# Attention's opening in a hybrid encoder block: the trunk's output buffer in another order, the exponential's table loaded ahead, the later keys split in two pieces

## The chip, the cores and the metric

The kernel runs on one core of a Trainium2 chip. A core has five engines with instruction streams of their own: TensorE (matrix products and transposes), VectorE, ScalarE (activation functions), GpSimd, and SyncE, which here only issues transfers. They are ordered by semaphores alone. In profile rows they are PE (PEld for its weight loads), DVE, ACT, POOL and SP; SPq and ACTq are the issues of transfers from the queues of SyncE and ScalarE. The metric is the device time of one execution in microseconds.

## The reference

One layer of a streaming encoder for a prompt of 2048 positions and a sample of 32 new positions on 1024 past ones. Everything is float32.

```python
(aq, ak, av, iq, ik, iw, za, uv, zb, glu, zc, gates) = split_columns(rms_norm(x, norm_g) @ w_in)
...
o_a = dsa_prompt(q, iq, iw, k, v, ik)                      # or dsa_attend with the cache
o_b, v_rows = gmlp_unit(uv, g_ln_g, g_ln_b, g_ws, g_bs)
o_c, conv_tail = conv_module(glu, left, c_w, c_b, c_ln_g, c_ln_b)
merged = (ga * ((o_a * jax.nn.silu(za)) @ w_a) + gb * ((o_b * jax.nn.silu(zb)) @ w_b)
          + gc * ((o_c * jax.nn.silu(zc)) @ w_c))
x = x + merged @ w_out
x = x + jax.nn.sigmoid(rms_norm(x, ple_g) @ w_pg) * (p @ w_ple)
```

The part in question is `dsa_attend`: 8 query heads of width 64 share 2 key and value heads, each query sees the 256 keys that an indexer selected, with a distance penalty per head:

```python
logits = jnp.einsum('btgrd,btkgd->btgrk', qg, kg).astype(jnp.float32) * (A_HEAD_DIM ** -0.5)
logits = logits - slopes[None, None, :, :, None] * dist[:, :, None, None, :]
logits = jnp.where(valid[:, :, None, None, :], logits, -jnp.inf)
prob = jax.nn.softmax(logits, axis=-1).astype(v.dtype)
out = jnp.einsum('btgrk,btkgd->btgrd', prob, vg)
```

## The kernel before, in words

The trunk (`stage_trunk`) multiplies the normed input with w_in in 59 jobs of 128 columns, each over five spans of 416 positions. Each float32 operand is split into a high and a low part, and a product is three matmuls. ScalarE copies each span from PSUM to its place in `j_out` (`evacuate`), span r to place r, and stores it to `T_dram`; from the third job on spans 0 and 1 go in one store and spans 2 to 4 in another. The last job stores 0 and 1, then 2 and 3, then 4, with a semaphore of its own for the last (`last_stored`). `stored[1]` counts the first kind, `stored[4]` the second.

Attention (`stage_attend`) follows. It works in 34 groups: a group is one tile of queries and one of the two key heads (four query heads), in the order of tiles 0, 3, 4, 1, 5, 2, 6, 7 and so on; tile t sees 128 (t + 1) keys. For each head of a group TensorE multiplies queries and keys (lines 2417 and 2418), VectorE adds the distances and takes the running minimum in one pass into the buffer `a_l` (line 2547), ScalarE takes the exponential in place (line 2473), TensorE transposes 128 columns of four heads at a time (line 2374), ScalarE copies the high part (`a_pthi`, line 2482), VectorE makes the low part (`a_ptlo`, line 2571), and TensorE multiplies with the values (lines 2438 and 2439). Three PSUM banks go round for products and three for transposes. Products, minima and exponentials of a group are done beside the transposes and values of the group before it. The sums' reciprocals (lines 2559 and 2563) go through DRAM: SyncE stores them (`share`, line 2137) and loads them broadcast as `a_factor` (line 2143); GpSimd multiplies them with the gates and the output (lines 2258 and 2264). SyncE also loads the queries (`a_q`, lines 148 and 149) and the distances (`a_nd`, line 2166), and GpSimd splits the queries (lines 2249 and 2251). All of this stands in a fixed order on each engine's queue.

`a_l` of head 0 begins at byte 163584 of each partition, `j_out` at byte 157440, with 1664 bytes to a place. So the first 512 columns of head 0's `a_l` lie over places 3 and 4 of `j_out`, and no other head's does. The first product's minimum (group 0, head 0) therefore waits for stores of `j_out` (`wait_for_outputs`), and the first of group 2 also for the last store. One of the two queries buffers lies over the other places and is loaded by SyncE, which waits for all stores first.

Keys are split into high and low parts by ScalarE (a cast, `high`, line 2455) and VectorE (a subtraction, `split`, line 2513): the first 512 of each key head ahead of group 0, the other 1536 at the starts of groups 2 and 3; the values of the later positions at those of groups 5 and 6. `SPLITS_AT` holds this table. The buffers with the raw later keys (`a_krest`) lie in the columns from 512 on of `a_l` of heads 4 and 5.

Of the kernel before, what the change touches and what calls it, by code (L numbers as in the profile page):

```python
# [45 lines left out]
SPAN = 416  # L46
# [1304 lines left out]
def stage_trunk(c):  # L1351
# [68 lines left out]
    kv_stored = c.kv_stored  # L1420

    w_in = c.I["w_in"].rearrange("(k q) n -> q k n", q=P)
    w_second = out[:].rearrange("q b t -> q (b t)")[:, 0:D].rearrange("q (k n) -> q k n", k=KD)
    pT = [c.psum[:, 2 * p:2 * p + 2, :].rearrange("q b (k t) -> q (b k) t", k=4) for p in range(4)]
    turn_bank = lambda t: t if t in GROUPS[0] else t % 2
# [26 lines left out]
    c.wait_for_products = lambda eng: eng.wait_ge(bank_full, finished(SLOTS - 1))  # L1452
    c.wait_for_banks_read = lambda eng, b: eng.wait_ge(bank_read, sequence(SLOTS - 1, b) + 1)
    c.wait_for_outputs = lambda eng: wait_for_stored(eng, SLOTS - 1)
    c.wait_for_last_output = lambda eng: eng.wait_ge(last_stored, 16)
    c.wait_for_early = lambda eng: (eng.wait_ge(product, IH * len(parts(NS))), eng.wait_ge(nat_stored, 32))

# [105 lines left out]
    def scalar(act):  # L1563
# [19 lines left out]
        def evacuate(j, b):  # L1583
            q = sequence(j, b)
            r, slot, t0 = q % len(SPANS), JOBS[j][1], SPANS[b][0]
            act.wait_ge(bank_full, q + 1)
            if j < 2:
                if q == 0:
                    act.wait_ge(w_lo_done, 2)
                if q >= len(SPANS):  # L1590
                    act.wait_ge(stored[r], 16)
            elif j == 2:
                act.wait_ge(stored[r], 32)
            else:
                act.wait_ge(stored[1 if b < 2 else 4], 16 * j)
            if S_Q <= slot < S_K:
                c.wait_for_scale(act)
                act.activation(out[:, r, :], c.psum[:, bank_of(j, b), 0:SPAN], ACT.Identity, scale=c.scale[:, slot - S_Q:slot - S_Q + 1]
                               ).then_inc(bank_read, 1)
            else:  # L1600
                act.activation(out[:, r, :], c.psum[:, bank_of(j, b), 0:SPAN], FUNC[JOBS[j][2]]).then_inc(bank_read, 1)  # L1601
            if j < 2:
                act.wait_ge(bank_read, q + 1)
                act.dma_start(c.T_dram[slot, :, t0:t0 + SPAN], out[:, r, :]).then_inc(stored[r], 16)
            elif b in ((1, 3, 4) if j == SLOTS - 1 else (1, 4)):
                first, end = HELD[0 if b == 1 else 1]
                sem = stored[1 if b == 1 else 4]
                if j == SLOTS - 1 and b > 1:
                    first, end, sem = (first, 4, sem) if b == 3 else (4, end, last_stored)
                act.wait_ge(bank_read, q + 1)  # L1610
                act.dma_start(c.T_dram[slot, :, first * SPAN:end * SPAN], out[:, first:end, :].rearrange("q b t -> q (b t)")
                              ).then_inc(sem, 16)

        def relu(n):
# [338 lines left out]
def stage_attend(c):  # L1953
# [379 lines left out]


    splits = [(k_hi[g][:, 0:FIRST_KEYS], k_lo[g][:, 0:FIRST_KEYS], kraw[g][:], (c.k_full, 64)) for g in range(KVH)]
    splits += [(k_hi[g][:, FIRST_KEYS:], k_lo[g][:, FIRST_KEYS:], krest[g][:], (c.rest_full[g], 32)) for g in range(KVH)]
    for g in range(KVH):
        dst = v_p[:, HALF:, g, :]
        splits.append((dst[:, :, 0:HD], dst[:, :, HD:P], vraw[1][:, :, g * HD:(g + 1) * HD], (values_full, 16)))

    SECOND_ROWS_AT = ((last_prompt, 12), (groups[-1], 2))
    SPLITS_AT = {2: (2,), 3: (3,), 5: (4,), 6: (5,)}

    WIDE = next(group for group in groups if len(group.tiles) > HALF)
    assert WIDE.n > 7
    FIRST_KEYS_SPLIT, KEYS_SPLIT, VALUES_SPLIT = 1, 3, 5

    late_splits = [(ks_hi[g][:, PAST:], ks_lo[g][:, PAST:], new_k[g][:], P) for g in range(KVH)]
    for g in range(KVH):
# [13 lines left out]
    def tensor(pe):  # L2363
# [26 lines left out]
        def unit(group, unit):  # L2390
# [7 lines left out]
            if s == 0 and h == group.buffers[0]:  # L2398
                if group.n == 0:
                    c.wait_for_first_queries(pe)  # L2400
                    c.wait_for_early_cleared(pe)
                    c.wait_for_banks_read(pe, QK - 1)
                if group.i == 1:
                    c.wait_for_second_queries(pe)
                if group.i > 1:
                    pe.wait_ge(q_ready[group.p], splits_of_queries(group.i) + 1)
                if group.i == 1:
                    pe.wait_ge(operands, FIRST_KEYS_SPLIT + group.g)
                if group.i == 2:
                    pe.wait_ge(operands, KEYS_SPLIT + group.g)  # L2410
                if group.t == DT:
                    pe.wait_ge(late_ready, len(late_splits))
                    pe.wait_ge(cache_ready, len(CACHE_GROUPS))
# [37 lines left out]
    def scalar(act):  # L2451
# [8 lines left out]

        c.wait_for_early_cleared(act)
        c.wait_for_products(act)

        def first():
            high(0)
# [43 lines left out]
    def vector(vec):  # L2509
# [13 lines left out]
        def unit(group, unit):  # L2523
            h, s, a, w, b, nb, n = unit
            if n == 0:
                c.wait_for_swish_spans(vec)
                c.wait_for_outputs(vec)
            if n == 6:
                c.wait_for_swish(vec)
            if unit is groups[KVH].units[0]:  # L2530
                c.wait_for_last_output(vec)
            n_d = c.nd_first if group.i == 0 else nd[group.p]
            if s == 0 and group.packed:
                vec.wait_ge(rs_cleared, 1 + 4 * KVH)
# [1354 lines left out]
```

## Time and profile before

| | us |
|---|---|
| median of 3 executions | 2644.74 (2643.83 to 2645.25) |
| the profiled execution, its own time | 2642.72 |
| its span | 2640.7 |
| TensorE busy in it | 2591.1 (98%) |
| VectorE busy | 2054.9 (78%) |
| ScalarE busy | 1496.6 (57%) |
| GpSimd busy | 1537.0 (58%) |

The span is the time from the first to the last instruction of the profiled execution; its own time is 2.0 us longer. All positions in time below are microseconds from the span's start. The trunk's last matmul starts at 1530.79; attention's last groups end at about 1965. Busy time of TensorE is modelled for a pipeline, so 98% does not say that no faster order of the work exists. A row of a timeline gives the start, the duration, the engine, the line, the operation, what it writes and reads, and in brackets the idle time in front of it with what ended it.

### The profile page before, as it was taken

The page shows a single profiled execution, that of the slowest core. Times are in us where ns is not written, and L with a number is a line of the kernel's source. Part 1 is how long each engine was busy: PE and PEld are TensorE (multiplying, and loading weights), DVE is VectorE, ACT ScalarE, POOL GpSimd, SP SyncE. Part 2 cuts the span into 40 slices and gives each one's busy share as a digit, 9 for nine tenths or more (in the row PEclk, how much of TensorE's full clock was granted, in tenths as well). Part 3 has the DMA queues.
Part 4 walks back from the last instruction along what each step waited for, and adds up shares of the span by engine and source line. Part 5 has one row for each costly group of instructions (what it writes and reads, how often), then busy time and mean ns, then how long its engine had stood idle before and what let it go on. Part 6 is the DMA issues. An engine that isn't in the chain of part 4 may idle for free. (4 is left out here: it accounts for less than half of the span.)

```text
span 2640.7 us, 40128 instructions
## 1 busy us (share of the span) xinstructions
PE 2591.1 (98%) x13799; PEld 2410.3 (91%) x13799; DVE 2054.9 (78%) x3857; ACT 1496.6 (57%) x2550; POOL 1537.0 (58%) x1114
## 2 busy tenths in 40 slices
PE   8999999999999999999999988999999999999998
PEld 8999999999999999999999967878889999877886
DVE  6377799999999999998363568999977666657656
ACT  6377578686868787785222367777760101326553
POOL 1100187787878796889345558543347663976562
PEclk9999999999999999999999989999999999999999
DMA  5433333233433332323465564222138976642221
GB/s 181 129 118 128 120 102 118 99 114 109 132 107 122 99 122 88 114 88 123 132 209 167 178 171 115 80 66 70 54 129 316 351 264 212 230 158 100 95 85 57
DMA packets 279959, 359.94 MB, mean 136 GB/s; under 512 B 37905, under 2 KB 227985, under 8 KB 279117
## 3 DMA queue, kind: packets, MB, share of 16 engines
q1 hardware_dynamic: 171667, 219.73, 26.0%
q10 hardware_dynamic: 108090, 137.66, 15.0%
q8 instruction: 110, 1.80, 0.3%
q14 instruction: 92, 0.75, 0.1%
HBM read 216.94 MB, written 139.74 MB: 135 GB/s over the span
## 5 line engine op out<-in xcount | busy, mean ns | idle before, releaser
L1762 PE MATMUL psum<-hT_hi,j_whi 128*128 128x416 f32 x2432 | 864.9, 356 | 1.6 <-ACT j_out L1601 0.8
L1762 PE MATMUL psum<-hT_hi,j_wlo 128*128 128x416 f32 x2432 | 852.7, 351 | 0.0
L1762 PE MATMUL psum<-hT_lo,j_whi 128*128 128x416 f32 x2432 | 851.6, 350 | 0.0
L1314 POOL TENSOR_TENSOR v_y<-v_y,v_product 128x422 f32<-128x422 f32 x459 | 562.9, 1264 | 88.9 <-ACT v_product L1296 88.9
L449 DVE TENSOR_SCALAR_CACHE_REDUCE s_tie<-s_key,s_bits 128x640 bf16<-128x640 f32 (+14 forms) x352 | 464.3, 1319 | 12.3
L1762 PEld LDWEIGHTS psum<-hT_hi,j_whi 128*128 128x128 f32 x2432 | 456.2, 188 | 11.2 <-issue 2.6
L1762 PEld LDWEIGHTS psum<-hT_lo,j_whi 128*128 128x128 f32 x2432 | 457.4, 188 | 9.0 <-issue 1.6
L1762 PEld LDWEIGHTS psum<-hT_hi,j_wlo 128*128 128x128 f32 x2432 | 456.2, 188 | 5.5
L1296 ACT ACTIVATE v_product<-v_x,v_taps 128x422 f32<-128x422 f32 x510 | 303.1, 641 | 81.4 <-POOL v_y L1314 58.7
L1601 ACT ACTIVATE j_out<-psum 128x416 f32<-128x416 f32 x285 | 144.9, 509 | 323.4 <-PE psum L1762 312.2
L1521 POOL TENSOR_TENSOR j_wlo<-j_w,j_whi 128x1024 fp32r<-128x1024 f32 x59 | 143.8, 2437 | 313.8 <-ACT j_whi L1581 313.8
L2482 ACT ACTIVATE a_pthi<-psum 128x512 fp32r<-128x512 f32 x278 | 161.8, 596 | 91.9 <-PE psum L2374 90.1
L432 ACT ACTIVATE s_ajunk<-s_key,s_abits,s_asign 128x1280 uint8<-128x1280 bf16 (+7 forms) x112 | 192.4, 1718 | 14.0 <-ACT j_out L1601 11.0
L2571 DVE TENSOR_TENSOR a_ptlo<-psum,a_pthi 128x512 fp32r<-128x512 f32 x278 | 186.2, 682 | 11.1 <-ACT a_pthi L2482 10.9
L2374 PEld LDWEIGHTS psum<-ident,a_l 128*128 128x128 f32 x1106 | 133.1, 141 | 53.4 <-DVE a_ptlo L2571 25.3
L2374 PE MATMUL psum<-ident,a_l 128*128 128x128 f32 x1106 | 166.0, 276 | 13.5 <-DVE a_ptlo L2571 9.0
L3205 PE MATMUL psum<-f_whi,f_ahi 128*128 128x512 f32 x448 | 177.2, 395 | 1.1 <-issue 0.9
L3205 PE MATMUL psum<-f_wlo,f_ahi 128*128 128x512 f32 x448 | 174.7, 390 | 0.0
L3205 PE MATMUL psum<-f_whi,f_alo 128*128 128x512 f32 x448 | 174.5, 389 | 0.0
L2764 PE MATMUL psum<-m_ohi,m_wlo 128*128 128x416 f32 x480 | 169.4, 353 | 0.0
L2764 PE MATMUL psum<-m_ohi,m_whi 128*128 128x416 f32 x480 | 168.3, 351 | 0.8 <-issue 0.8
L2764 PE MATMUL psum<-m_olo,m_whi 128*128 128x416 f32 x480 | 167.5, 349 | 0.0
(372 smaller groups left out, 4947.0 us busy)
## 6 DMA issues: line engine op xcount, KB each, us to landing
T_dram<-j_out ACTq DMA_DIRECT2D x58, 624.0 KB, 2.9
j_w<-in_w_in ACTq DMA_DIRECT2D x59, 512.0 KB, 3.8
T_dram<-j_out ACTq DMA_DIRECT2D x60, 416.0 KB, 2.4
m_gate<-T_dram SPq DMA_DIRECT2D x60, 416.0 KB, 5.6
m_oraw<-B_dram SPq DMA_DIRECT2D x15, 832.0 KB, 8.6
M_dram<-m_merged ACTq DMA_DIRECT2D x10, 832.0 KB, 7.1
n_x<-in_x_prompt SPq DMA_DIRECT2D x16, 512.0 KB, 6.1
G_dram<-f_prepsums ACTq DMA_DIRECT2D x8, 1024.0 KB, 5.6
```

Of the source, the lines that this page charges most:

```text
L432: do(act.activation(a_junk[:, 0:n], tops, ACT.Sign, scale=a_sign[:, p:p + 1], bias=level, accum_out=a_cnt))
L449: do(vec.tensor_scalar(tie[:, 0:n], K[:, 0:n], bits[:].bitcast(F32), 0.0, ALU.is_ge, ALU.add, accum_out=cnt[:]))
L1296: act.activation(product[n % RING][:], x, ACT.Identity, scale=taps[:, k:k + 1]).then_inc(made, 1)
L1314: pool.tensor_tensor(y[k % 2][:], y[k % 2][:], product[n % RING][:], ALU.add).then_inc(added, 1)
L1521: pool.tensor_tensor(w_lo[j % 2][:], w_raw[:], f32(w_hi[j % 2][:]), ALU.subtract).then_inc(w_lo_done, 1)
L1601: act.activation(out[:, r, :], c.psum[:, bank_of(j, b), 0:SPAN], FUNC[JOBS[j][2]]).then_inc(bank_read, 1)
L1762: last = pe.matmul(bank, w[p][:, k, :], h[:, k, t0:t0 + SPAN], start=(k == 0 and q == 0), stop=(k == KD - 1 and q == 2))
L2374: last = pe.transpose(c.psum[0:w, PT[u], r * P:(r + 1) * P], L[h][:, block * P:block * P + w], c.ident[:])
L2482: act.activation(pT_hi[number % KEPT][0:w, 0:n], c.psum[0:w, PT[u], 0:n], ACT.Copy).then_inc(pt_hi, 1)
L2571: vec.tensor_tensor(pT_lo[number % KEPT][0:w, 0:n], c.psum[0:w, PT[u], 0:n], f32(pT_hi[number % KEPT][0:w, 0:n]), ALU.subtract).then_inc(p ...
L2764: last = pe.matmul(c.psum[:, n, 0:SPAN], wt[:, k, n * P:(n + 1) * P], o[u][:, k, :], start=(k == 0 and q == 0), stop=(k == 3 and q == 2))
L3205: last = pe.matmul(out, left[:, k, :], right[:, k, :], start=(k == 0 and x == 0), stop=(k == KH - 1 and x == 2))
```

## The change

Three edits. The output buffer's places are turned by three: span r lies at place (r + 3) mod 5, so spans 0 and 1 lie at places 3 and 4, and spans 2, 3, 4 at 0, 1, 2. The first minimum waits for `stored[0]` and `stored[1]` only, and the wait ahead of group 2 goes. ScalarE runs an exponential of one column into a constant that is not needed any more, as soon as the trunk's products are finished. The 1536 later keys are split 512 (up to position 1024) and 1024: the first piece where it was, the second at the starts of groups 12 and 13, ahead of the first group that needs it (tile 8, group 16).

```diff
+    place = lambda r: (r + 3) % len(SPANS)
...
+    c.wait_for_first_outputs = lambda eng: (eng.wait_ge(stored[0], 32), eng.wait_ge(stored[1], 16 * SLOTS))
...
-                act.activation(out[:, r, :], c.psum[:, bank_of(j, b), 0:SPAN], FUNC[JOBS[j][2]]).then_inc(bank_read, 1)
+                act.activation(out[:, place(r), :], c.psum[:, bank_of(j, b), 0:SPAN], FUNC[JOBS[j][2]]).then_inc(bank_read, 1)
...
-                act.dma_start(c.T_dram[slot, :, first * SPAN:end * SPAN], out[:, first:end, :].rearrange("q b t -> q (b t)")
+                act.dma_start(c.T_dram[slot, :, first * SPAN:end * SPAN], out[:, place(first):place(end - 1) + 1, :].rearrange("q b t -> q (b t)")
...
-    splits += [(k_hi[g][:, FIRST_KEYS:], k_lo[g][:, FIRST_KEYS:], krest[g][:], (c.rest_full[g], 32)) for g in range(KVH)]
+    NEAR = SEQ // 2
+    piece = lambda g, a, b: (k_hi[g][:, a:b], k_lo[g][:, a:b], krest[g][:, a - FIRST_KEYS:b - FIRST_KEYS], (c.rest_full[g], 32))
+    splits += [piece(g, FIRST_KEYS, NEAR) for g in range(KVH)]
...
+    splits += [piece(g, NEAR, SEQ) for g in range(KVH)]
...
-    SPLITS_AT = {2: (2,), 3: (3,), 5: (4,), 6: (5,)}
+    SPLITS_AT = {2: (2,), 3: (3,), 5: (4,), 6: (5,), 12: (6,), 13: (7,)}
+    FAR_KEYS = next(group for group in groups if group.keys > NEAR)
...
+                if group.i == FAR_KEYS.i:
+                    pe.wait_ge(operands, FAR_SPLIT + group.g)
...
         c.wait_for_early_cleared(act)
         c.wait_for_products(act)
+        act.activation(c.scale[:, 0:1], c.zero[:], ACT.Exp)
...
             if n == 0:
                 c.wait_for_swish_spans(vec)
-                c.wait_for_outputs(vec)
+                c.wait_for_first_outputs(vec)
             if n == 6:
                 c.wait_for_swish(vec)
-            if unit is groups[KVH].units[0]:
-                c.wait_for_last_output(vec)
```

ScalarE at the end of the trunk, before: the last store, the table's load, the exponentials of group 0.

```order
L1601 ACTIVATE j_out<-psum 128x416
L1611 DMA T_dram<-j_out 128x416
L2473 ACT_TABLE_LOAD
L2473 ACTIVATE a_l_232,a_sums<-a_l_232,a_lows 128x128
L2473 ACTIVATE a_l_233,a_sums<-a_l_233,a_lows 128x128
```

And in the changed kernel:

```order
L1603 ACTIVATE j_out<-psum 128x416
L1613 DMA T_dram<-j_out 128x416
L2472 ACT_TABLE_LOAD
L2472 ACTIVATE scale<-zero 128x1
L2483 ACTIVATE a_l_232,a_sums<-a_l_232,a_lows 128x128
L2483 ACTIVATE a_l_233,a_sums<-a_l_233,a_lows 128x128
```

The table's load now belongs to the one-column activation, whose operands are there, and no longer to the first exponential, which waits for the first minimum.

VectorE at the start of group 12, before: the low part of the group's first transposed block, reciprocal and its transpose, then minima (two rows each) and low parts by turns.

```order
L2571 TENSOR_TENSOR a_ptlo_248<-psum,a_pthi_244 128x512
L2559 RECIPROCAL a_rs<-a_sums 128x4
L2563 STREAM_TRANSPOSE a_rsT_260<-a_rs 128x32
L2547 ISA a_l_237,a_lows<-psum,a_nd_230,a_lows 128x448
L2547 ISA a_lows 128x1
L2571 TENSOR_TENSOR a_ptlo_249<-psum,a_pthi_245 128x512
```

And in the changed kernel:

```order
L2579 TENSOR_TENSOR a_ptlo_248<-psum,a_pthi_244 128x512
L2523 TENSOR_TENSOR a_klo_222<-a_krest_174,a_khi_220 128x1024
L2567 RECIPROCAL a_rs<-a_sums 128x4
L2571 STREAM_TRANSPOSE a_rsT_260<-a_rs 128x32
L2555 ISA a_l_237,a_lows<-psum,a_nd_230,a_lows 128x448
L2555 ISA a_lows 128x1
L2579 TENSOR_TENSOR a_ptlo_249<-psum,a_pthi_245 128x512
```

One subtraction of 1024 columns has come in ahead of the reciprocal; group 13 has another at the same place, and the corresponding rows of groups 2 and 3 read 128x512 where they read 128x1536. SyncE's, GpSimd's and TensorE's rows stand in the order of before.

## Rows read from the trace of the kernel before

**Rows 1.** Windows: us, then busy us and instructions by engine, granted clock, DMA.

```profile
1534.00:1548.00 14.00, 11.99 (x36) 8.69 (x37) 10.48 (x34) 10.42 (x31) 9.24 (x6) 0.52 0.59 151
...
1640.00:1660.00 20.00, 19.69 (x113) 15.91 (x112) 18.79 (x48) 16.62 (x32) 15.28 (x11) 1.00 0.45 122
```

**Rows 2.** Timeline of the opening: start, duration, engine, operation, idle time in front.

```profile
1531.73 0.35 ACTq L1611 DMA_DIRECT2D T_dram<-j_out  x1
...
1533.62 0.29 DVE L2547 CUSTOM_DVE_ANT_0 a_l<-psum,a_ndfirst 128x128 f32<-128x128 f32 x1 [7.83 <-DMA T_dram<-j_out]
...
1534.02 1.28 ACT L2473 ACT_TABLE_LOAD   x1 [2.32 <-DVE a_lows L2547]
...
1537.90 0.59 ACT L2482 ACTIVATE a_pthi<-psum 128x512 fp32r<-128x512 f32 x1
```

**Rows 3.** The store of 1527.2, the last swish store's issue, SyncE's wait behind it.

```profile
L1611 ACTq DMA_DIRECT2D T_dram<-j_out x1: 327/327/327, 1527.2 to 1527.2; - x1
...
DMA to landing us min/median/max: 5.9/5.9/5.9
...
1525.15 0.51 SPq L902 DMA_DIRECT2D B_dram<-w_y  x1
...
SPq L925 <- DMA B_dram<-w_y: 6.7, 1, 6.7
```

**Rows 4.** Source view, lines 2513 and 2455: ns min/median/max, first and last start.

```profile
L2513 DVE TENSOR_TENSOR a_klo<-a_kraw,a_khi x2: 970/1366/1762, 1537.6 to 1538.5; 128x512 fp32r<-128x512 f32 x2
L2513 DVE TENSOR_TENSOR a_klo<-a_krest,a_khi x2: 1747/2072/2396, 1550.3 to 1561.1; 128x1536 fp32r<-128x1536 f32 x2
L2513 DVE TENSOR_TENSOR a_vp<-a_vraw,a_vp x2: 682/784/887, 1577.3 to 1584.2; 128x512 fp32r<-128x512 f32 x2
...
L2455 ACT CAST a_khi<-a_kraw x2: 602/608/613, 1536.9 to 1537.4; 128x512 fp32r<-128x512 f32 x2
L2455 ACT CAST a_khi<-a_krest x2: 1456/1466/1475, 1547.6 to 1556.9; 128x1536 fp32r<-128x1536 f32 x2
```

**Rows 5.** Timeline at group 2's start, VectorE and GpSimd.

```profile
1549.73 0.69 DVE L2571 TENSOR_TENSOR a_ptlo<-psum,a_pthi 128x512 fp32r<-128x512 f32 x1 [1.42 <-ACT a_pthi L2482]
...
1549.85 1.27 POOL L2264 TENSOR_TENSOR a_oa<-a_oa,a_factor 64x512 f32<-64x512 f32 x1
...
1550.33 2.40 DVE L2513 TENSOR_TENSOR a_klo<-a_krest,a_khi 128x1536 fp32r<-128x1536 f32 x1
```

**Rows 6.** SyncE's issues in order of time; last, the values' landing.

```profile
1538.14 0.43 SPq L2182 DMA_DIRECT2D a_vraw<-out_v_prompt  x1
1540.60 1.27 SPq L2137 DMA_DIRECT2D RS_dram<-a_rsT  x4
1545.64 0.47 SPq L2143 DMA_DIRECT2D a_factor<-RS_dram  x1
...
1562.90 0.64 SPq L149 DMA_DIRECT2D a_q<-T_dram  x1
...
1583.28 0.59 SPq L2166 DMA_DIRECT2D a_nd<-ND_dram  x1
...
a_vraw<-out_v_prompt SPq DMA_DIRECT2D x1, 512.0 KB, 6.8
```

**Rows 7.** Timeline: what waits for these queries and distances.

```profile
1567.17 1.90 POOL L2249 TENSOR_TENSOR a_qs<-a_q,zero 128x1024 fp32r<-128x1024 f32 x1 [10.25 <-DMA a_q<-T_dram]
...
1587.16 0.56 DVE L2547 CUSTOM_DVE_ANT_0 a_l<-psum,a_nd 128x384 f32<-128x384 f32 x1 [0.94 <-DMA a_nd<-ND_dram]
```

**Rows 8.** Timeline at group 12's start; last, a wait of VectorE in 1628 to 1652.

```profile
1628.62 1.28 POOL L2273 TENSOR_TENSOR a_oa<-a_oraw,a_oa 64x512 f32<-64x512 f32 x1
...
1629.53 0.17 DVE L2559 RECIPROCAL a_rs<-a_sums 128x4 f32<-128x4 f32 x1
...
1630.12 0.68 DVE L2547 CUSTOM_DVE_ANT_0 a_l<-psum,a_nd,a_lows 128x448 f32<-128x448 f32 x1 [0.17 <-PE psum L2418]
...
DVE a_ptlo L2571 <- ACT a_pthi L2482: 0.3, 1, 0.3
```

More of the change, by code:

```diff
@@ L1597, in evacuate @@
                 c.wait_for_scale(act)
-                act.activation(out[:, r, :], c.psum[:, bank_of(j, b), 0:SPAN], ACT.Identity, scale=c.scale[:, slot - S_Q:slot - S_Q + 1]
+                act.activation(out[:, place(r), :], c.psum[:, bank_of(j, b), 0:SPAN], ACT.Identity, scale=c.scale[:, slot - S_Q:slot - S_Q + 1]
                                ).then_inc(bank_read, 1)
             else:
-                act.activation(out[:, r, :], c.psum[:, bank_of(j, b), 0:SPAN], FUNC[JOBS[j][2]]).then_inc(bank_read, 1)
+                act.activation(out[:, place(r), :], c.psum[:, bank_of(j, b), 0:SPAN], FUNC[JOBS[j][2]]).then_inc(bank_read, 1)
             if j < 2:
                 act.wait_ge(bank_read, q + 1)
-                act.dma_start(c.T_dram[slot, :, t0:t0 + SPAN], out[:, r, :]).then_inc(stored[r], 16)
+                act.dma_start(c.T_dram[slot, :, t0:t0 + SPAN], out[:, place(r), :]).then_inc(stored[r], 16)
             elif b in ((1, 3, 4) if j == SLOTS - 1 else (1, 4)):
@@ L2339, in stage_attend @@
         splits.append((dst[:, :, 0:HD], dst[:, :, HD:P], vraw[1][:, :, g * HD:(g + 1) * HD], (values_full, 16)))
+    splits += [piece(g, NEAR, SEQ) for g in range(KVH)]
     SECOND_ROWS_AT = ((last_prompt, 12), (groups[-1], 2))
-    SPLITS_AT = {2: (2,), 3: (3,), 5: (4,), 6: (5,)}
+    SPLITS_AT = {2: (2,), 3: (3,), 5: (4,), 6: (5,), 12: (6,), 13: (7,)}
+    FAR_KEYS = next(group for group in groups if group.keys > NEAR)
+    assert FAR_KEYS.g == 0 and FAR_KEYS.n - KVH > 13
     WIDE = next(group for group in groups if len(group.tiles) > HALF)
     assert WIDE.n > 7
-    FIRST_KEYS_SPLIT, KEYS_SPLIT, VALUES_SPLIT = 1, 3, 5
+    FIRST_KEYS_SPLIT, KEYS_SPLIT, VALUES_SPLIT, FAR_SPLIT = 1, 3, 5, 7
     late_splits = [(ks_hi[g][:, PAST:], ks_lo[g][:, PAST:], new_k[g][:], P) for g in range(KVH)]
```

## The prediction

> **What bounds the kernel now.** The windows view by stretches comes first. From 1534 to 1548 us, the opening of attention, TensorE is granted 0.52 of its clock (almost wholly its 1.2 GHz level) and nobody is full; from 1640 to 1660 TensorE is busy 19.69 and VectorE 18.79 of 20 us [rows 1]. So the opening is a chain of waits, and later attention runs two full engines in step. Behind attention everything is ordered by semaphores and nothing starts at a fixed time, so what attention gains or loses is the change of the total.
>
> The timeline of the opening shows the first minimum starting at 1533.62 after 7.83 us of idle time that a store of j_out ended; the exponential's table is loaded from 1534.02, for 1.28 us, once that minimum is there; the first a_pthi copy starts at 1537.90 [rows 2].
>
> The timeline of SyncE and GpSimd is where I spent most time, because an opening that gets faster has to be fed. SyncE issues the second half of the values at 1538.14 (6.8 us to landing), the first reciprocal stores at 1540.60, the first factor load at 1545.64, the second half of the fourth tile's queries at 1562.90 and the distances of the fifth tile at 1583.28 [rows 6]. GpSimd idles 10.25 us until those queries have landed, at 1567.17; VectorE idles 0.94 us at 1587.16 for those distances, which had been issued only 3.9 us before [rows 7].
>
> **The change part by part.**
>
> *Fewer stores to wait for.* The first minimum no longer waits for the store that carries spans 2 and 3 of the last job. That store was issued at 1527.2 and landed 5.9 us later, 1533.1 [rows 3]; VectorE moved 0.5 us behind it. What is late next is the wait that stays in the same instruction's list, for the swish stage's stores: SyncE issued the last of these until 1525.66 and then waited 6.7 us, until 1532.36 [rows 3]. With the same 0.5 us behind it the first minimum starts at 1532.9, 0.7 us earlier. Bounds: 0 (if the swish stores land later than here) and 1.3 (no lag at all). The wait for the last span's store, dropped before the second tile's minima, cost nothing: they run some microseconds later than it lands. The buffer's other order moves no instruction in the trunk and keeps each store one contiguous piece: nothing either way.
>
> *Table ahead.* ScalarE is free from 1532.08, when its last store is issued (1531.73 plus 0.35) [rows 2]. The table stands at 1533.4 instead of 1535.30. The added one-column activation is shorter than the 0.61 us of a 512-column cast [rows 4] and lies where ScalarE idled. The exponentials can start 1.5 us earlier or so, but TensorE still has five pairs of products to run behind the first minimum before it transposes, and these move by 0.7 only. The first a_pthi copy, which needs both, moves between 0.7 and 1.7 us; I take 1.3.
>
> *Later keys in two pieces.* In groups 2 and 3 (each group is a tile and half of the heads) the cast takes 0.61 instead of 1.47 us, the subtraction 0.68 (the 512-column values piece without anything beside it) instead of 2.40 and 1.75 [rows 4]. In group 2 VectorE had waited 1.42 us for the a_pthi copy that stands behind the cast, so these 0.86 us pass through, then 2.40 - 0.68 = 1.72; in group 3 I count 1.75 - 0.68 = 1.07 in full (its lower bound is 0). Gross gain of the opening: 1.3 + 0.86 + 1.72 + 1.07 = 4.95 us by 1563.
>
> *What is late next.* None of these 4.95 us is in SyncE's and GpSimd's chain. Its links from 1540.60 on are: reciprocals landing, factor load at 1545.64, ten more issues, reciprocals again, queries at 1562.90, GpSimd from 1567.17 with hardly a pause (one split of queries, two groups of gates), a store of attention's output, reciprocals, distances at 1583.28. In it I find waits for transfers and for GpSimd, and one for VectorE, at its head: the 1540.60 issue. If VectorE arrives 1.3 us earlier there, the four small stores go out 1.3 us earlier, but behind 512 KB of values issued at 1538.14 that landed at 1544.94; SyncE went on at 1545.64, 0.7 us behind that landing and 3.8 us behind its own last small store (1540.60 plus 1.27) [rows 6]. So I let this chain move by 0.3 us (bounds 0 and 1.3). The minimum at 1587.16 is the first to read those distances and VectorE runs in order. Whatever the opening gained above 0.3 us is waited away there.
> The Trainium skill (DMA: Bandwidth & Descriptors, section Queues, rings and completion order) says that a ring's descriptors are consumed in order and that a semaphore's increment lands after the engine's earlier writes. By it the chain would move by 0; with a fixed latency from issue it would be the 1.3.
>
> *The pieces that come back.* Two casts and two subtractions of 1024 columns now stand at the starts of groups 12 and 13, at 1629.53 and some 11 us later. No row shows that width; halfway between 0.68 (512) and 1.75 (1536) is 1.21 us, which is the lower bound. The subtraction at 1550.33 began while GpSimd ran an operation from 1549.85 to 1551.12, and ended at 1552.73, 1.6 us after that end [rows 5]: it stood still first. At 1628.62 GpSimd starts 1.28 us of the same sort, so group 12's piece would stand still until 1629.90, 0.37 us [rows 8]. For group 13 the bounds are 0 and the 1.90 us of GpSimd's queries operation [rows 7]; I take 0.8. Together 2 x 1.21 + 0.37 + 0.8 = 3.6 us (bounds 2.4 and 6.2).
> The Trainium skill (SBUF — State Buffer, section Who interferes with whom) says that a VectorE instruction with two SBUF inputs and a GpSimd instruction that reads SBUF lock each other out, the second one waiting for the whole of the first. The four short pieces and the long ones here agree with that; by the rule with no such overlap the sum would be 2.4.
> What hides them? Behind the place in group 12 VectorE idles 0.17 us, and over 1628 to 1652 it waited 0.3 us for ScalarE [rows 8]: 0.5 us. TensorE waits for the a_ptlo right behind it, and has itself no more than some tenths to spare [rows 1]. So 3.1 us come through (bounds 1.2, with every microsecond of VectorE's idle time used, and 6.2). The casts, about 1.0 us, fit into ScalarE's waits.
>
> *Sum.* -0.3 + 3.1 = +2.8 us; I shade this to +2.5, since queue slack that rows don't show can only help. The profiled execution took 2642.72 us, so 2645.2; the median before is 2644.74, 2.0 above it, so 2647.2 us as measured.
>
> **The rivals.**
> - *The factor chain moves with VectorE.* Fixed latency, 1.3 us instead of 0.3: +1.5 us, 2646.2. For it: the 3.8 us after the issue's end are long and named as a wait for these stores alone. Against it: the landing of the values 0.7 us before.
> - *The late pieces are hidden.* VectorE's busy 18.79 of 20 leave 1.2 us; if the rings between TensorE and VectorE take up both pieces, what remains is some 0.5 us: +0.2, 2644.9. Against: TensorE is full too, and it waits for this very engine.
> - *Faster: the distances at 1583.28 are not what holds.* This is one mechanism: SyncE's chain gives way to an earlier VectorE, because its links are shorter with less traffic beside them. It decides from the point where it moves by more than 3.1 us; were all 4.95 us passed on, the time would be 4.95 - 3.1 = 1.9 us below before, 2642.8. For it: the wait at 1587.16 is only 0.94 us. Against: each link is a transfer or a GpSimd operation that no edit touches.
> - *Clock.* The opening ran at the 1.2 GHz level behind a lull of TensorE. Waiting for 1587 makes TensorE's lull longer and could drop it again. With TensorE busy nine tenths of the time later on [rows 1], 4 us at half rate lose 2 us of products, 2649.2. The reverse (a shorter lull at 1532 keeps the clock up) gains nothing at 1587.
>
> **How the numbers follow.** Forecast 0.45, factor chain 0.15, hidden pieces 0.15, faster 0.15, clock 0.10. The range from 2642.6 to 2649.6 reaches from the faster case to the clock's; beyond it lie the bound of 6.2 us and a part of the faster case. 0.2% is 5.3 us, about what a measurement of this kernel can tell from no change. No case's centre is that far: faster 0.02, same 0.94, slower 0.04. Inside it only one case, of 0.15, lies below before.
>
> **What would show it.** First minimum near 1532.9 and the table load before it; in groups 2 and 3 subtractions of 0.7 to 1 us; SyncE's factor load still within 0.5 us of 1545.64 and the distances within 1 us of 1583.28; a VectorE wait for a_nd of 2 us or more before 1587; the 1024-column pieces at 1.2 us or, beside GpSimd, up to 3, with TensorE waiting behind them. I am wrong if the distances are issued 2 us earlier, or if group 14 starts no later than before.

## The result and the profile after

The kernel before takes 2643.59 us in the runs that share a chip with the changed one (median of 20), the changed kernel 2647.76 us (median of 20, 2645.97 to 2654.89). The ratio is 1.0015 with a 95% interval of [1.0009, 1.0022], so the change costs 4.0 us, between 2.4 and 5.8. One of the 20 executions of before took 4109.26 us; the ratio is formed of fast runs alone, without it. The forecast was 2647.2 us, +2.5. The profiled executions took 2648.93 us after and 2642.72 before.

The windows view of the changed kernel: us, then busy us and instructions of PE, PEld, DVE, ACT and POOL, granted clock, DMA share, GB/s.

```profile
1534.00:1548.00 14.00, 11.28 (x43) 7.75 (x42) 10.31 (x32) 10.30 (x33) 9.71 (x8) 0.76 0.63 157
1570.00:1580.00 10.00, 7.03 (x30) 6.18 (x31) 4.88 (x13) 4.25 (x9) 9.22 (x10) 0.66 0.32 90
1640.00:1660.00 20.00, 17.26 (x92) 13.70 (x91) 17.44 (x40) 13.26 (x25) 14.27 (x10) 0.91 0.24 65
```

The kernel before from 1570 to 1580:

```profile
1570.00:1580.00 10.00, 8.59 (x54) 6.67 (x53) 9.15 (x27) 9.33 (x22) 8.05 (x10) 1.00 0.43 115
```

Against [rows 1] the opening has a higher clock, 0.76 for 0.52. There is a new hole from 1570 to 1580, where VectorE is busy for 4.88 of 10 us instead of 9.15 and the clock is 0.66 instead of 1.00, and a second one from 1640 to 1660, where TensorE falls from 19.69 to 17.26 of 20 and its clock from 1.00 to 0.91.

The opening's timeline, as [rows 2]. In this execution attention's first product starts at 1532.07 and in that of before at 1530.98, so 1.09 us have to be taken off each start before the two are compared.

```profile
1532.81 0.35 ACTq L1613 DMA_DIRECT2D T_dram<-j_out  x1
1533.21 0.29 DVE L2555 CUSTOM_DVE_ANT_0 a_l<-psum,a_ndfirst 128x128 f32<-128x128 f32 x1 [6.34 <-SPq L925]
1533.25 1.28 ACT L2472 ACT_TABLE_LOAD   x1 [0.47 <-ACT j_out L1603]
...
1534.54 0.20 ACT L2472 ACTIVATE scale<-zero 128x1 f32<-128x1 f32 x1
...
1536.04 0.29 DVE L2555 CUSTOM_DVE_ANT_0 a_l<-psum,a_ndfirst 128x128 f32<-128x128 f32 x1 [0.87 <-SPq L927]
...
1537.22 0.58 ACT L2492 ACTIVATE a_pthi<-psum 128x512 fp32r<-128x512 f32 x1
```

The table no longer waits for a minimum, and the first copy to a_pthi comes 5.15 us after the first product instead of 6.92. The first minimum comes 1.14 us after it instead of 2.64. What releases the first minimum is now SyncE's wait for the swish stores (L925), and its wait for the tails (L927) holds the seventh for another 0.87 us.

Groups 2 and 3, as [rows 4, 5]: the new 512-column pieces.

```profile
1548.30 0.69 DVE L2579 TENSOR_TENSOR a_ptlo<-psum,a_pthi 128x512 fp32r<-128x512 f32 x1 [0.89 <-ACT a_pthi L2492]
...
1548.91 0.68 DVE L2523 TENSOR_TENSOR a_klo<-a_krest,a_khi 128x512 fp32r<-128x512 f32 x1
...
1557.81 0.68 DVE L2523 TENSOR_TENSOR a_klo<-a_krest,a_khi 128x512 fp32r<-128x512 f32 x1
```

Then SyncE, GpSimd and VectorE, as [rows 6, 7]: the links of the chain and the waits that end it.

```profile
1540.05 2.06 SPq L2139 DMA_DIRECT2D RS_dram<-a_rsT  x4
1546.32 0.47 SPq L2145 DMA_DIRECT2D a_factor<-RS_dram  x1
...
1563.90 1.53 SPq L149 DMA_DIRECT2D a_q<-T_dram  x1
...
1568.60 1.90 POOL L2251 TENSOR_TENSOR a_qs<-a_q,zero 128x1024 fp32r<-128x1024 f32 x1 [11.84 <-DMA a_q<-T_dram]
...
1572.97 0.58 PE L2426 MATMUL psum<-a_khi,a_qs 128*128 128x256 f32 x1 [3.71 <-POOL a_qs L2253]
...
1575.23 0.42 DVE L2555 CUSTOM_DVE_ANT_0 a_l<-psum,a_nd 128x256 f32<-128x256 f32 x1 [3.67 <-PE psum L2427]
...
1584.61 0.59 SPq L2168 DMA_DIRECT2D a_nd<-ND_dram  x1
...
1588.70 0.56 DVE L2555 CUSTOM_DVE_ANT_0 a_l<-psum,a_nd 128x384 f32<-128x384 f32 x1 [1.01 <-DMA a_nd<-ND_dram]
```

Counted from the first product, the factor load comes 0.41 us earlier than before and the distances 0.24 us later. The chain has hardly moved, so VectorE, which was 5.5 us ahead at group 3's reciprocal, stands still for 3.67 us at 1575 and twice more by 1588.70. TensorE idles 3.71 us there for the queries that GpSimd is splitting, and its clock falls behind that lull: this is the 0.66 of the window. Part of the lead is lost to slower products, then, and not to the wait itself. At 1588.70 it is 1.54 us behind before's 1587.16, of which 1.09 is the later start.

The starts of groups 12 and 13, as [rows 8]:

```profile
1631.12 1.24 DVE L2523 TENSOR_TENSOR a_klo<-a_krest,a_khi 128x1024 fp32r<-128x1024 f32 x1
1631.24 2.27 POOL L2260 TENSOR_TENSOR a_factor<-a_factor,a_za 64x512 f32<-64x512 f32 x1
1632.28 0.17 DVE L2567 RECIPROCAL a_rs<-a_sums 128x4 f32<-128x4 f32 x1
...
1642.33 1.89 POOL L2251 TENSOR_TENSOR a_qs<-a_q,zero 128x1024 fp32r<-128x1024 f32 x1
1642.64 2.66 DVE L2523 TENSOR_TENSOR a_klo<-a_krest,a_khi 128x1024 fp32r<-128x1024 f32 x1
1644.30 3.22 POOL L2253 TENSOR_TENSOR a_qs<-a_q,a_qs 64x1024 fp32r<-64x1024 f32 x1
...
1647.03 1.08 PE L2381 MATMUL psum<-ident,a_l 128*128 128x128 f32 x4 [2.61 <-DVE a_ptlo L2579]
```

The piece of group 12 takes 1.24 us. That of group 13 begins 0.31 us behind a GpSimd operation that reads SBUF, and ends 1.08 us after that one's end: it stood still first. TensorE then idles 2.61 us, and its next four products (transposes, line 2381) take 1.08 us.

Reciprocals of group 8, counted from the first product, and the stretch from there to group 14's are the two measures used below. Before: 67.43 and 52.21 us. After: 67.90 and 57.16. Nearly all of the loss lies in the second, 4.95 us against 0.47. Both are measures of one execution each.

### The profile page after: what moved, and what is told of

It is laid out like the page before. It is cut to its first block and busy times, and to the rows that moved or that the text cites. A ratio compares the mean times of both kernels' runs of the same rounds, so it can differ in the third digit from the quotient of the medians.

```text
span 2647.1 us, 40131 instructions
## 1 busy us (share of the span) xinstructions
PE 2592.4 (98%) x13799; PEld 2411.2 (91%) x13799; DVE 2060.4 (78%) x3859; ACT 1496.2 (57%) x2553; POOL 1538.3 (58%) x1114
## 5 line engine op out<-in xcount | busy, mean ns | idle before, releaser
L1523 POOL TENSOR_TENSOR j_wlo<-j_w,j_whi 128x1024 fp32r<-128x1024 f32 x59 | 149.4, 2532 | 321.4 <-ACT j_whi L1583 321.4
```

The lines of the kernel that those rows point to most:

```text
L1523: pool.tensor_tensor(w_lo[j % 2][:], w_raw[:], f32(w_hi[j % 2][:]), ALU.subtract).then_inc(w_lo_done, 1)
```

## The experiments

All were timed in five rounds against the kernel before on the same chip; "against before" is worked out from the ratio and its interval. Theory A is the prediction's: the opening's gain is waited away, and the loss is the late pieces.

**1. The change without the split of the keys.**

```
-    splits += [piece(g, FIRST_KEYS, NEAR) for g in range(KVH)]
+    splits += [(k_hi[g][:, FIRST_KEYS:], k_lo[g][:, FIRST_KEYS:], krest[g][:], (c.rest_full[g], 32)) for g in range(KVH)]
...
-    splits += [piece(g, NEAR, SEQ) for g in range(KVH)]
...
-    SPLITS_AT = {2: (2,), 3: (3,), 5: (4,), 6: (5,), 12: (6,), 13: (7,)}
+    SPLITS_AT = {2: (2,), 3: (3,), 5: (4,), 6: (5,)}
```

> The change without its split of the keys: the output places, the wait for two stores and the early load of the table stay, the keys beyond the first 512 are made in one piece per group again. Theory A (the opening's gain of the first minima and of the table, 1.5 to 1.8 us here, is waited away by 1589 at the queries and distances of the third and fourth tile, and the loss comes from the 1024-column pieces at groups 12 and 13): 2643.6, no further than 1 us from before; the idle time of VectorE between 1568 and 1589 is 1 to 2 us larger than before's. Theory B (the changed order of the output buffer costs the trunk 1 us, as the later first product in the profile of after suggests): +1 us, with the first product of attention 1 us later than before's 1530.98 again. Theory C (the opening's gain survives and only the split costs): -1.3 us, 2642.3.

Measured: 2643.31 us, ratio 1.0001 [0.9992, 1.001], +0.3 us (-2.1 to +2.6). Its first minimum:

```profile
1534.81 0.29 DVE L2548 CUSTOM_DVE_ANT_0 a_l<-psum,a_ndfirst 128x128 f32<-128x128 f32 x1 [8.08 <-SPq L925]
```

It comes 2.89 us after its first product, no earlier than before's 2.64, though the wait for the j_out store is gone: the swish store landed later here. The first product is at 1531.92, which looked like theory B, but in six of the later kernels with the same output places it is at 1530.31 to 1531.02. In two others, numbers 5 and 10, it is at 1536.00 and 1535.29; in the four profiled executions with the old places it is at 1530.79 to 1531.26. So theory B has no support in the time, whose interval does hold its +1, and it is not excluded. The stretch from group 8 to 14 is 52.21 us. Group 8's reciprocal is at 68.29 us, 0.86 later than before's, so nothing of the opening's gain is left there. Theory A stands; C's -1.3 lies inside the interval of the time.

**2. The split alone, on the kernel before.**

```
+    splits += [piece(g, NEAR, SEQ) for g in range(KVH)]
...
-    SPLITS_AT = {2: (2,), 3: (3,), 5: (4,), 6: (5,)}
+    SPLITS_AT = {2: (2,), 3: (3,), 5: (4,), 6: (5,), 12: (6,), 13: (7,)}
```

> The kernel before with the split of the keys alone: pieces of 512 at groups 2 and 3, of 1024 at groups 12 and 13. Theory A: the whole loss is here, +3.5 to +4.5 us over before (2647 to 2648), with the sum of VectorE's piece at group 13 stretched to over 2.3 us while GpSimd splits queries, and group 14's reciprocal 4.5 to 5.5 us later than before's. Theory B (the trunk pays): +2.5 to +3. Theory D (the 5.8 us seen at group 14 in the one profile was an accident of that execution's clock; pieces cost their bare 1.2 us each): +1 to +2.

Measured: 2649.12 us, ratio 1.0017 [1.0008, 1.0025], +4.5 us (+2.1 to +6.6). Groups 8 to 14 take 57.36 us, 5.15 more than before; group 14's reciprocal is 6.9 us later than before's, where A said 4.5 to 5.5. A wait takes the gain of groups 2 and 3:

```profile
1587.35 0.56 DVE L2554 CUSTOM_DVE_ANT_0 a_l<-psum,a_nd 128x384 f32<-128x384 f32 x1 [3.81 <-DMA a_nd<-ND_dram]
...
1642.85 2.66 DVE L2520 TENSOR_TENSOR a_klo<-a_krest,a_khi 128x1024 fp32r<-128x1024 f32 x1
```

The whole loss is in the split, as A said. Theory D's +1 to +2 is out.

**3. The late pieces at groups 10 and 12.**

```
-    SPLITS_AT = {..., 12: (6,), 13: (7,)}
+    SPLITS_AT = {..., 10: (6,), 12: (7,)}
```

> The change, with the two 1024-column pieces put at groups 10 and 12 in place of 12 and 13, so that neither begins beside GpSimd's split of queries, which runs at odd groups. If the lock at group 13 and the lull behind it are what cost (theory A): each piece takes 1.2 to 1.3 us on VectorE, no wait of TensorE over 1.5 us follows either, the TensorE clock stays at 1.00, and the time is +2 to +2.7 over before instead of +4. If the cost is a piece's bare work on a full VectorE (theory D): as after, within 0.5 us (+3.5 to +4.5).

Measured: 2646.60 us, ratio 1.0012 [1.0003, 1.002], +3.2 us (+0.8 to +5.3). The profile tells more than the time:

```profile
1615.18 1.85 DVE L2523 TENSOR_TENSOR a_klo<-a_krest,a_khi 128x1024 fp32r<-128x1024 f32 x1
...
1630.71 2.12 DVE L2523 TENSOR_TENSOR a_klo<-a_krest,a_khi 128x1024 fp32r<-128x1024 f32 x1
```

Neither piece took the 1.2 to 1.3 us expected, since GpSimd has shorter operations at even groups too, and TensorE waited 1.67 and 1.74 us behind them where no wait over 1.5 was expected. But the clock stays at 1.00 in 1640 to 1660 and groups 8 to 14 take 55.04 us, 2.1 less than in after. The expectation for the pieces was wrong. The interval of the time holds A's loss of 2 to 2.7 and D's of 3.5 to 4.5 alike; the profile's 2.8 us over before in groups 8 to 14 lies by A's.

**4. The fourth tile's queries loaded earlier.**

```
             share(sp, first)
-            if 0 < i < TILES - 2:
+            if 1 < i < TILES - 2:
                 load_queries(i + 2)
...
+            if i == 0:
+                load_queries(3)
             share(sp, second)
```

> The change, with the third tile's queries loaded by SyncE in the first tile's shares instead of behind the second tile's (their buffer is free from the start), so GpSimd splits them some 10 us earlier. Theory A (at 1575 the products of the fourth tile in order wait for these queries, which hold back what the opening gained): the 3.67 us wait of VectorE at 1575 goes or falls under 1 us; the distances at 1588 then hold, with a wait longer by as much unless their load is also earlier; time 0 to 2.5 us below after (+1.5 to +4 over before), the low clock around 1575 gone. Rival (the distances alone hold, as the prediction had it): the wait moves whole to 1588 and the time is after's within 0.5 us.

Measured: 2647.53 us, ratio 1.0015 [1.0006, 1.0024], +4.0 us (+1.6 to +6.3).

```profile
1575.02 0.42 DVE L2557 CUSTOM_DVE_ANT_0 a_l<-psum,a_nd 128x256 f32<-128x256 f32 x1 [3.98 <-DMA a_nd<-ND_dram]
...
1642.43 2.67 DVE L2525 TENSOR_TENSOR a_klo<-a_krest,a_khi 128x1024 fp32r<-128x1024 f32 x1
...
1646.84 0.63 PE L2383 MATMUL psum<-ident,a_l 128*128 128x128 f32 x4 [2.61 <-DVE a_ptlo L2581]
```

Neither expectation was met: the wait did not go, and it did not move to 1588. It keeps its place and nearly its size, but what ends it is now the fourth tile's distances: SyncE issues those behind the same shares of reciprocals. Both queries and distances had been late by about 4 us. By accident this execution also measures the clock. After the same piece and the same lull of 2.61 us, TensorE's four products take 0.63 us where after's took 1.08; the clock in 1640 to 1660 is 1.00, and group 13's to group 14's reciprocal takes 10.36 us against 11.90 in after (10.38 in before).

**5. The late pieces put into the wait, at group 4** (the list of pieces is put in the same order).

```
-    SPLITS_AT = {2: (2,), 3: (3,), 5: (4,), 6: (5,), 12: (6,), 13: (7,)}
+    SPLITS_AT = {2: (2,), 3: (3,), 4: (4, 5), 5: (6,), 6: (7,)}
```

> The change, with both 1024-column pieces put at the start of group 4 (about 1566), ahead of the 4 to 5 us in which VectorE waits around 1571 to 1577 for the fourth tile in order. Theory A (the opening's gain is waited away there, so that stretch has room): the two pieces fill the wait, VectorE's wait at 1575 falls from 3.67 us to under 1.5, groups 12 to 14 run as before, and the time is before's within 1 us (-1 to +1). Rival (the pieces delay what the SyncE chain itself waits for, group 4's reciprocal at 1566 and group 5's at 1579): +3 to +5, the wait at 1588 grown.

Measured: 2643.55 us, ratio 0.9999 [0.999, 1.0008], -0.3 us (-2.6 to +2.1).

```profile
1570.33 2.35 DVE L2523 TENSOR_TENSOR a_klo<-a_krest,a_khi 128x1024 fp32r<-128x1024 f32 x2
...
1580.04 0.69 DVE L2579 TENSOR_TENSOR a_ptlo<-psum,a_pthi 128x512 fp32r<-128x512 f32 x1 [0.95 <-ACT a_pthi L2492]
```

Both pieces take 2.35 us together and the 3.67 us wait is gone (this execution's attention starts at 1536.00). Groups 8 to 14 take 52.20 us. The same instructions that cost 5 us on full engines cost nothing that the time can tell in the hole that the change itself had opened. They may not be quite free: in this one execution group 8's reciprocal is at 69.49 us, 1.6 later than after's.

**6. Queries and distances ahead of the shares, in all tiles.**

```
+            if 0 < i < TILES - 2:
+                load_queries(i + 2)
             share(sp, first)
-            if 0 < i < TILES - 2:
-                load_queries(i + 2)
...
+            if 0 < i < TILES - 2:
+                load_distances(i + 2)
             share(sp, second)
-            if 0 < i < TILES - 2:
-                load_distances(i + 2)
```

> The change, with SyncE's load of a later tile's queries put ahead of the first share of reciprocals of each tile, and its load of the distances ahead of the second share, in all tiles; nothing is removed. Theory A (queries and distances behind the shares are the one thing that eats the opening's gain): no wait of VectorE over 1 us on a_nd or for the queries' products between 1565 and 1592; group 8's reciprocal, 1599.97 in the profile of after, 4 to 5 us earlier; the losses at groups 12 and 13 stay (5.0 us in after's profile); time 2643 to 2644.5, -1 to +1 against before. Rival 1 (another chain is right behind, GpSimd's split or the factor of the outputs): gain under 1.5 us, time +2.5 to +4. Rival 2 (the earlier loads disturb other work): +4 or more.

Measured: 2644.98 us, ratio 1.0006 [0.9997, 1.0015], +1.6 us (-0.8 to +4.0). No wait of VectorE above 1 us between 1565 and 1592 is left, and group 8's reciprocal stands at 64.08 us, 3.8 earlier than after's 67.90. Groups 8 to 14 still take 56.91. This is where the opening's gain had gone; rival 1 is out by the profile, though the time's interval alone reaches it. The time, expected at -1 to +1, came out at +1.6; its interval holds both.

**7. The late low halves on GpSimd.**

```
+    FAR_AT = (10, 12)
...
+            if group.n in FAR_AT:
+                far(FAR_AT.index(group.n))
...
+            pool.tensor_tensor(lo, src, f32(hi), ALU.subtract).then_inc(far_made, 1)
```

> The change, with the low halves of the two 1024-column pieces made by GpSimd ahead of its work of groups 10 and 12 and the casts by ScalarE a group earlier; VectorE has neither piece. If the loss is VectorE's time for them (theory A): groups 9 to 14 cost what they cost in the kernel before, within 0.5 us, and the time is +0.3 to -1 against before. If a split of keys anywhere beside the groups costs (GpSimd's own delay, as its outputs of groups 9 and 11 come 2 to 3 us later): +2 to +4.

Measured: 2642.63 us, ratio 0.9997 [0.9988, 1.0006], -0.8 us (-3.2 to +1.6).

```profile
1586.67 0.56 DVE L2567 CUSTOM_DVE_ANT_0 a_l<-psum,a_nd 128x384 f32<-128x384 f32 x1 [4.08 <-DMA a_nd<-ND_dram]
...
1614.27 2.40 POOL L2293 TENSOR_TENSOR a_klo<-a_krest,a_khi 128x1024 fp32r<-128x1024 f32 x1
...
1634.19 2.43 POOL L2293 TENSOR_TENSOR a_klo<-a_krest,a_khi 128x1024 fp32r<-128x1024 f32 x1 [1.16 <-POOLq L3807]
```

Groups 8 to 14 take 52.20 us: GpSimd's 4.8 us cost nothing there. This edit changes two things, the engine and the groups, since the pieces stand at 10 and 12. Number 3 has those groups with VectorE and lost 2.8 us in the same stretch, so by these single profiles the engine is worth those 2.8 us and the rest of the 5 went with the place. The wait before the distances is whole again, 4.08 us.

**8. Both: the diffs of 6 and 7 together.**

> Both of the last two together: SyncE's loads of queries and distances ahead of the shares, and the 1024-column low pieces on GpSimd. Theory A: the opening's gain is neither waited away at 1575 to 1589 nor given back at groups 12 and 13: -4 to -5 us against before, 2638.5 to 2639.5, about the sum of the two single effects. Rival (a third place takes it): no better than -1.5.

Measured: 2639.08 us, ratio 0.9983 [0.9975, 0.9992], -4.5 us (-6.6 to -2.1). It is faster than both kernels. Group 8's reciprocal is at 64.54 us and groups 8 to 14 take 52.21, as the two single kernels had it. By these measures of one execution each the gain is 2.9 us; its profiled execution took 2639.39 us, 3.3 less than before's. Of the 4.1 us gained by group 3, some are still lost, in the values' piece of group 6:

```profile
1573.22 0.68 DVE L2535 TENSOR_TENSOR a_vp<-a_vraw,a_vp 128x512 fp32r<-128x512 f32 x1
...
1580.08 2.72 DVE L2535 TENSOR_TENSOR a_vp<-a_vraw,a_vp 128x512 fp32r<-128x512 f32 x1
```

GpSimd, fed earlier, was splitting queries from 1577.93 to 1582.25.

**9. The early loads alone, on the kernel before** (the diff of 6).

> The kernel before with SyncE's loads of queries and distances ahead of the shares, and nothing of the change. Theory A (the loads behind the shares matter where the opening has gained; before lost 0.94 us to them at 1587 and nothing elsewhere): the wait at 1587.16 goes, group 8's reciprocal is 0.5 to 1 us earlier than before's 1598.41 when counted from attention's first product, time -0.5 to -1.2. Rival (the early loads are worth 2 us or more by themselves, and the change's opening is worth less than the sum says): -2 or lower.

Measured: 2643.24 us, ratio 0.9996 [0.9987, 1.0005], -1.1 us (-3.4 to +1.3). The wait at 1587 is gone but nothing is gained by group 8: 69.07 us, 1.6 later than before. The values' piece took 2.23 us (before: 0.68 and 0.89) and VectorE waited 1.58 us for products at 1586.24. TensorE's clock fell there as well: 0.57 in the four microseconds from 1582. A's reason for the gain is not borne out; its number and the rival's both lie inside the interval.

**10. The opening's two edits with the early loads, keys whole** (the diffs of 1 and 6 together).

> The output places, the wait for two stores and the early table load, with the early loads of queries and distances, and the keys beyond 512 in one piece as before. Theory A: the opening's 1.3 us (group 0's reciprocal counted from the first product: 8.1 us with these edits in seven profiled executions, 9.3 without in two) now survive to group 8 with the 0.94 us of the wait at 1587: -1.5 to -2.5. Rival (the opening's gain is lost at group 2, where ScalarE's longer casts hold): -0.5 to -1.2, as the kernel before with the early loads.

Measured: 2642.70 us, ratio 0.9997 [0.9988, 1.0005], -0.8 us (-3.2 to +1.3). Group 8's reciprocal is at 67.39 us, as in before. A missed; by group 4 the kernel was 1.0 us ahead and lost it again by group 5, so the rival's reason (a loss at group 2) fails too. Both numbers lie inside the interval.

**11. Split, GpSimd pieces and early loads without the opening's edits** (the diffs of 2, 6 and 7 together).

> The kernel before with the keys split, the 1024-column low pieces on GpSimd and the early loads, without the output places, the wait for two stores and the early table load. Theory A: the near pieces' 3 us at groups 2 and 3 survive, the opening's 1.3 us are missing against the version that has everything (2639.08): -3 to -4, 2640 to 2641. Rival (the opening's edits are worth nothing once the swish store lands late): as the version with everything, -4.5 to -5.5.

Measured: 2639.48 us, ratio 0.9983 [0.9974, 0.9992], -4.5 us (-6.9 to -2.1). Group 8's reciprocal is at 64.62 us against 64.54 in number 8, though group 0's is 0.95 us later (9.42 against 8.47). The rival is nearer, though A's -3 to -4 lies inside the interval too. Four pairs of kernels differ in the opening's edits alone. By the time against before, with and without them: +0.3 and 0, -0.8 and -1.1 (10 and 9), +4.0 and +4.5 (after and 2), -4.5 and -4.5 (8 and 11). At group 8's reciprocal the edits put the same pairs 0.86 us later, then 1.68, 1.26 and 0.08 earlier. So the edits move the time by 0.5 us or less, far inside its intervals, and the single profiles scatter by more than that. What number 8 keeps comes from groups 2 and 3.

**12. Number 8 with both values' pieces at group 5.**

```
-    SPLITS_AT = {2: (2,), 3: (3,), 5: (4,), 6: (5,)}
+    SPLITS_AT = {2: (2,), 3: (3,), 5: (4, 5)}
```

> The version with everything (the change, early loads, the 1024-column low pieces on GpSimd: 2639.08, -4.95), with the second piece of the values' split made at group 5 too, where GpSimd had a free stretch, in place of group 6. In that version's trace VectorE's piece of group 6 took 2.72 us, from 1580.08 to just behind the end of GpSimd's a_q split at 1582.25, where the same piece at group 5 took 0.68. Theory L (an operation of VectorE with both inputs in SBUF stands until GpSimd's split that is under way has ended): both pieces at group 5 together 1.3 to 1.5 us, group 8's reciprocal counted from attention's first product 64.5 falls to 62.5 to 63.0, time -6 to -7 against before. Rival (TensorE's wait of 2.2 us for GpSimd's queries at 1582 would hold anyway): no gain over that version, -4.5 to -5.5, and the wait for a_qs stays.

Measured: 2641.63 us, ratio 0.9993 [0.9984, 1.0002], -1.9 us (-4.2 to +0.5).

```profile
1572.28 1.28 DVE L2535 TENSOR_TENSOR a_vp<-a_vraw,a_vp 128x512 fp32r<-128x512 f32 x2
...
1578.83 0.70 SPq L2169 DMA_DIRECT2D a_nd<-ND_dram  x1
...
1583.45 1.05 PE L2391 MATMUL psum<-ident,a_l 128*128 128x128 f32 x4
...
1584.54 0.56 DVE L2567 CUSTOM_DVE_ANT_0 a_l<-psum,a_nd 128x384 f32<-128x384 f32 x1 [3.52 <-DMA a_nd<-ND_dram]
```

Theory L was right on the pieces, 1.28 us for both, and wrong on the time: VectorE came to the fifth tile 3.5 us before its distances, whose first reader starts 5.7 us after their issue. The wait is back because the load is still ordered by SyncE's other work, not because an instruction is slow. Nor was the rival's number met, though its wait for a_qs stays: 2.13 us here, 2.23 in number 8. The profile shows where number 12 falls behind number 8. At the first minimum of the fifth tile it is 0.5 us behind, at group 8's reciprocal 1.8 (66.38 against 64.54). Between them its clock is down for a time: after nearly the same lull its four transposes take 1.05 us where number 8's take 0.60, and from 1580 to 1590 the clock is 0.66 against 1.00. Whether the other executions lost their time in the same way, no trace shows.

## Why the prediction was right, step by step

It was right in sign and within its range, and the two main mechanisms are borne out: the opening's gain is waited away, and the late pieces cost time. The change moved the time by 4.0 us where it said 2.5. That 2647.2 and the measured 2647.76 lie within 0.6 us is luck: the forecast started from 2644.74 us, and the kernel before measured beside the changed one takes 2643.59.

*Fewer stores to wait for: 0.7 us earlier.* Only sometimes. In after it was 1.50 us, more than the upper bound of 1.3. From the first product to the first minimum the four profiled executions with the old wait took 2.64 to 3.09 us. The ten with the new one took 1.14, 1.40 and 2.31 in three, and 2.89 to 3.26 in seven. The last swish store decides, and it lets the minimum go 7.0 to 9.1 us after its issue. The lower bound of 0, "if the swish stores land later than here", was the usual case. The seventh minimum's wait for the tails (0.87 us in after) was not in the prediction.

*Table ahead: exponentials 1.5 us earlier, first a_pthi 1.3.* Right in size; in after itself the a_pthi moved by 1.77. Counted from the first product, the first a_pthi stands at 6.92 to 7.37 us in the four without the edits and at a median of 6.0 in the ten with them, 1.2 earlier. What is left of it at group 8 is too little for the times to tell, as the four pairs under number 11 show.

*Two pieces at groups 2 and 3: 0.86 + 1.72 + 1.07.* Right: casts of 0.60 us, pieces of 0.68 each in after. By group 3's reciprocal after was 5.5 us ahead of before, counted from the first product, for a forecast of 4.95 by a little later. In four of the ten kernels that have these pieces the first took 1.1 to 1.6 us beside GpSimd.

*What is late next: the chain moves by 0.3 us.* Right: 0.41 at the factor load, -0.24 at the distances. The Trainium skill (DMA: Bandwidth & Descriptors, section Queues, rings and completion order) would have it at 0, and a fixed latency from the issue at 1.3; the trace lies by the first. Counted from the first product, the small stores' issue came 1.64 us earlier in after than in before, and the factor load only 0.41. The fourteen profiled executions fit the first reading. The first factor load is issued 0.66 to 0.79 us behind the landing of the second half of the values in twelve of them, and 0.30 and 0.15 in numbers 2 and 5. Behind the end of the small stores' issue it comes 3.05 to 5.34 us. So the load seems to follow the values and not the stores; no run moved the values to test it. The place was only half right. I put the whole wait at 1587 with "2 us or more" for a_nd there; it was 1.01, and 3.67 and 1.42 had gone at 1575 and 1577. There the fourth tile's queries and distances, behind the same shares, came late too. I had looked at the last reader alone. Over the kernels with the keys split and nothing put into the wait, whose queries or distances still stand behind the shares, the big wait lies at 1575 (after, 3, 4) or 1587 (2, 7) and is 3.7 to 4.5 us long.

*The late pieces: 3.6 us, 3.1 after what is absorbed.* This term was mis-sized: 4.95 us in after (57.16 against 52.21), 5.15 in number 2. The bare piece was right, 1.24 us against 1.21, and group 12 cost 1.2. Group 13 cost 2.2 up to its reciprocal, with a stand of about 1.4 us where 0.8 was taken. The 0.5 us of slack absorbed nothing. And the clock fell behind the lull that the piece makes: 11.90 us from group 13 to 14 against 10.36 in number 4, which had the lull and kept the clock, so 1.5 us.

*The rivals.* The factor chain did not move by 1.3, and the pieces were not hidden. The clock case had the mechanism and came true in part. The wait did bring the clock down, at 1575 and not at 1587 (0.66 from 1570 to 1580), and at group 8 after is 0.5 us behind before where -0.3 was forecast. No run parts that wait from its clock. The lull in group 13, which it did not name, brought it down once more. The faster case is turned down for this kernel by every wait above, and number 8 makes it true by taking away both of its conditions.

*Sum.* -0.3 + 3.1 became, by the profile, +0.5 + 4.95 = 5.4 us from the first product to group 14. The timed runs say 4.0 [2.4, 5.8]. The profiled execution may have been a costlier one than most; number 4 shows how 1.5 us can be absent. How often the clock falls in the timed runs, nothing here shows.

## What to carry to other kernels

Before moving work out of a chain of waits, list every transfer that the faster stretch will ask for, and where its issue stands in the queue's program: here a gain of some 4 us was waited away until two loads were moved ahead of stores that had nothing to do with them. Work that is moved away must be weighed where it lands: the same two subtractions cost 5 us on VectorE at groups 12 and 13, 2.8 at groups 10 and 12, and nothing that the time can tell in the wait at group 4 or on GpSimd. A fix is only worth what the work in front of it has gained: the early loads brought group 8 forward by 3.8 us behind the short pieces (number 6 against after), and not at all with the keys whole (number 9 is 1.6 us later than before there, number 10 level with it).

## What the runs showed of the hardware

- VectorE's operations with two inputs in SBUF and GpSimd's stretch each other both ways. VectorE's piece of group 13 took 2.66 us for 1.24, and two of GpSimd's operations that met such a piece took 2.27 us for 1.28 and 3.22 for 2.40. The rule of the Trainium skill (SBUF — State Buffer, section Who interferes with whom) agrees with it: the second waits for the whole of the first.
- The granted clock does not always fall behind the same lull. After 2.6 us without work, the four products took 1.08 us in after and in number 2 (1.09), and 0.63 in number 4; the windows gave 0.91, 0.91 and 1.00. After 2.2 us (number 8) it stayed at 1.00, and after 2.1 (number 12) it fell within 2 us. A term of 1.5 us can thus be in one execution and absent from the next.
- The start of attention moves by up to 5.7 us between profiled executions of kernels with the same trunk and the same output places (first product at 1530.31 to 1536.00), so each stage has to be counted from its own start.
